# One change to the paged-decode phase of a two-layer decoder step: value products over two periods, low parts shared out anew, key and value loads in turn

## The reference, cut to what matters

```python
k_past = cache_k[page_table].reshape((db, past_len) + cache_k.shape[2:])
v_past = cache_v[page_table].reshape((db, past_len) + cache_v.shape[2:])
...
s = jnp.einsum('bqhcd,bkhcd->bhcqk', q, kp).astype(F32) * ATTN_SCALE
...
p = jax.nn.softmax(jnp.concatenate(scores, axis=-1), axis=-1)
w = p[:, :, 0] - lam * p[:, :, 1]
...
o = jnp.einsum('bhqk,bkhe->bqhe', w[..., start:start + s_len].astype(vp.dtype), vp)
```

## Time and profile before

| | us |
|---|---|
| median of 3 runs | 1853.9 (1852.12 to 1858.34) |
| the profiled execution's own time | 1853.4 |
| its span in the trace | 1851.5 |
| decode, from its first load to the next phase's first | 1446.7 to 1733.2 in the span |

### The profile page before, as it was taken

One profiled execution on the slowest core, in us unless ns is written; L12 is line 12 of the kernel. 1 busy time (PEld: TensorE's weight loads), 2 busy tenths in 40 slices (PEclk: granted clock), 3 DMA queues, 4 the chain that ended last, 5 costly groups with the idle time before them and its releaser, 6 DMA issues. The chain is left out here.

```text
span 1851.5 us, 31191 instructions
## 1 busy us (share of the span) xinstructions
PE 1684.9 (91%) x9243; PEld 1371.8 (74%) x9243; DVE 1041.6 (56%) x2696; ACT 839.0 (45%) x1994; POOL 319.6 (17%) x814
## 2 busy tenths in 40 slices
PE   5299999999999997988999999999999688887798
PEld 4288888888888876768878778778788566665576
DVE  4534445445454443354777767767766477776443
ACT  5333444344443332242555545555545366666322
POOL 1011212212112120010122221222222012111101
PEclk8599999999999998998999999999999799899799
DMA  6122050350421104322221211211101577877713
GB/s 167 27 58 69 27 94 2 92 94 0 94 49 44 38 2 143 100 83 66 58 57 44 66 54 37 61 54 43 43 12 35 187 253 250 293 239 249 264 53 112
DMA packets 164757, 171.97 MB, mean 93 GB/s; under 512 B 14634, under 2 KB 133834, under 8 KB 164658
## 3 DMA queue, kind: packets, MB, share of 16 engines
q1 hardware_dynamic: 161538, 170.78, 31.1%
q10 hardware_dynamic: 3120, 0.01, 0.1%
HBM read 141.85 MB, written 28.91 MB: 92 GB/s over the span
## 5 line engine op out<-in xcount | busy, mean ns | idle before, releaser
L1016 PE MATMUL PS<-WH,XH 128*128 128x512 f32 x512 | 212.5, 415 | 0.0
L1016 PE MATMUL PS<-WH,XL 128*128 128x512 f32 x512 | 201.9, 394 | 0.0
L1016 PE MATMUL PS<-WL,XH 128*128 128x512 f32 x512 | 201.9, 394 | 0.0
L1996 PE MATMUL PS<-W,XH 128*128 128x512 f32 x384 | 123.8, 403 | 0.0
L1750 ACT ACTIVATE WORK<-PD,WORK 128x896 f32<-128x896 f32 (+7 forms) x128 | 95.0, 742 | 62.8 <-DVE WORK L1917 57.9
L1016 PEld LDWEIGHTS PS<-WH,XL 128*128 128x128 f32 x512 | 96.2, 188 | 22.9
L1016 PEld LDWEIGHTS PS<-WH,XH 128*128 128x128 f32 x512 | 96.8, 189 | 19.8
L1016 PEld LDWEIGHTS PS<-WL,XH 128*128 128x128 f32 x512 | 96.8, 189 | 17.2
L1916 DVE TENSOR_REDUCE WORK<-PD 128x1 f32<-128x896 f32 (+7 forms) x128 | 96.4, 753 | 4.2 <-issue 2.0
L1996 PE MATMUL PS<-WH,XH 128*128 128x512 f32 (+2 forms) x224 | 85.7, 383 | 3.1 <-ACT WH L1715 3.1
L843 DVE SCALAR_TENSOR_TENSOR WORK<-PS,WORK 128x128 f32<-128x128 f32 (+1 forms) x72 | 20.1, 279 | 119.6 <-PE PS L1042 118.4
(11 more groups left out here) (365 smaller groups left out, 4663.5 us busy)
## 6 DMA issues: line engine op xcount, KB each, us to landing
RAW<-in_cache_k SPq DMA_DIRECT2D x64, 512.0 KB, 4.7
WORK<-in_cache_v SPq DMA_DIRECT2D x64, 512.0 KB, 4.5
RAW<-in_w_in_a SPq DMA_DIRECT2D x40, 512.0 KB, 7.3
out<-WORK SPq DMA_DIRECT2D x16, 512.0 KB, 3.0
out<-RAW SPq DMA_DIRECT2D x16, 512.0 KB, 3.2
RAW<-in_w_in_b SPq DMA_DIRECT2D x60, 128.0 KB, 2.4
RAW<-in_w_kv SPq DMA_DIRECT2D x56, 128.0 KB, 2.3
WORK<-d_G SPq DMA_DIRECT2D x8, 528.0 KB, 12.2
```

Source lines behind the costliest of these rows:

```text
L1016: last = nc.tensor.matmul(bank, x[:, k, tok(t, P)], wkvoz(w)[:, k, :], start=(k == i == 0), stop=(k == KT - 1 and i == 2))
L1996: last = nc.tensor.matmul(out, x[:, k, at(NT - 1 - s)], w[:, k, cols], start=(k == i == 0), stop=(k == KT - 1 and i == 2))
```

## The change

TensorE, ScalarE and VectorE get orders of their own. TensorE multiplies value pages 0 to 3 of batch b - 1 in period b, as before, and pages 4 to 7 and the new values only in period b + 1, between the turns of that period; so there is one more, short period at the end. ScalarE cuts the value pages between the key pages, from the period's start, and takes the result out in the middle of a period. GpSimd makes the low parts of pages 0, 2, 3, 4, 6 and 7, VectorE those of 1 and 5. The rota of banks has W after turn 7 and not after turn 9. SyncE loads keys and values in turn, page by page. The page table is loaded in the gates phase instead of at the start of decode, and the first eight key loads no longer wait for the small turns at decode's start (the inputs of these turns land in value places instead of the key places' tile).

```diff
@@ gates_phase, block.sync
+                    sp.dma_start(PT[:, :], page_table.rearrange("b n -> (b n)").unsqueeze(0)).then_inc(g_st, 16)
...
-                        sp.wait_ge(g_st, 64)
+                        sp.wait_ge(g_st, 80)
@@ decode_phase
-            TURNS = [u for u in range(10)] + ["W"] + [u for u in range(10, 16)]
+            TURNS = [u for u in range(8)] + ["W"] + [u for u in range(8, 16)]
...
+            ON_DVE = (1, 5)
+            ON_POOL = tuple(p for p in range(PAGES) if p not in ON_DVE)
+            def low_made(eng, i, p):
+                group, s = (ON_DVE, vld) if p in ON_DVE else (ON_POOL, vl)
+                wait(eng, s, len(group) * i + group.index(p) + 1)
+            PE_ORDER = ("T0", "V4", "V5", "T1", "V6", "T2", "V7", "N", "T3", "S0", "W", "S1",
+                        "T4", "V0", "T5", "V1", "T6", "V2", "T7", "S2", "V3", "S3")
+            ACT_ORDER = ("Q", "K0", "V0", "E", "K1", "V1", "K2", "V2", "K3", "V3", "O", "W",
+                         "K4", "V4", "K5", "R0", "V5", "K6", "V6", "K7", "R1", "V7", "R2")
+            DVE_ORDER = ("Q", "K0", "K1", "E", "V1", "K2", "K3", "W", "K4", "R0", "V5", "K5", "K6", "K7", "R1", "R2", "M")
...
-                body(0, True, False)
-                with eng.Fori(1, DB) as b:
+                body(0)
+                body(1)
+                with eng.Fori(2, DB) as b:
...
-                body(DB, False, True)
+                body(DB)
+                body(DB + 1)
@@ block.sync
-                    sp.dma_start(PT[:, :], page_table.rearrange("b n -> (b n)").unsqueeze(0)).then_inc(d_pt, 16)
-                    for j, dst in enumerate((RAW[0:TS, 4 * D - D:4 * D], RAW[0:TS, 4 * D:5 * D], AVS[0:TS, :])):
+                    for j, dst in enumerate((VB[0:TS, 2, :], VB[0:TS, 3, :], AVS[0:TS, :])):
...
-                    sp.wait_ge(d_pt, 16)
-                    sp.wait_ge(pre, 1)
...
+                    def body(b):
+                        for p in range(4, PAGES):
+                            keys(b, p)
+                            values(b - 1, p)
+                        if has_rest(b):
+                            store(b - 2)
+                        for p in range(4):
+                            keys(b + 1, p)
+                            values(b, p)
@@ block.gpsimd
-                        for p in (3, 7):
+                        for p in ON_POOL:
@@ block.scalar, v_high
-                            wait(act, av, PAGES * i + max(p - 3, 0))
+                            wait(act, av, PAGES * i + p - 3)
...
+                        def outputs():
+                            act.wait_ge(avd, i)
+                            wait(act, d_avs, 16 * (i - 1))
@@ block.tensor
-                        def value(p):
+                        def value(j, p):
+                            low_made(pe, j, p)
...
+                            elif step[0] == "V" and int(step[1]) < 4 and has_weights(b):
+                                value(i, int(step[1]))
+                            elif step[0] == "V" and int(step[1]) >= 4 and has_rest(b):
+                                value(i - 1, int(step[1]))
```

More of the change, by code:

```diff
@@ L2150, in sequences, with has_keys, has_weights @@
                     if links:
-                        links.enter(b - 1, per)
-                    body(b, True, True)
+                        links.enter(b - 2, per)
+                    body(b)
                 if links:
-                    links.leave(DB - 1)
-                body(DB, False, True)
+                    links.leave(DB - 2)
+                body(DB)
+                body(DB + 1)
+            def has_keys(b):
+                return not isinstance(b, int) or b < DB
+            def has_weights(b):
+                return not isinstance(b, int) or 1 <= b <= DB
@@ L2157, in wait, with has_rest @@
+            def has_rest(b):
+                return not isinstance(b, int) or b >= 2
             def wait(eng, s, count):
@@ L2179, in keys, with values @@
                           .then_inc(k_ld[p % 4], 16)
[L2181 to L2188, removed]
+                    def values(i, p):
+                        if p >= 4:
+                            low_made(sp, i, p - 4)
+                        else:
+                            low_made(sp, i - 1, p + 4)
                         src = cache_v[page(sp, i * PAGES + p), :, :, :]
@@ L2202, in _ @@
                         keys(1, p)
[L2203 to L2213, removed]
+                        if p == 2:
+                            sp.wait_ge(pre, 1)
+                        values(0, p)
+                    body(1)
+                    with sp.Fori(2, DB - 1) as b:
+                        body(b)
                     for p in range(4, PAGES):
                         keys(DB - 1, p)
-                    for p in range(4, PAGES):
                         values(DB - 2, p)
-                    for p in range(4):
+                    store(DB - 3)
+                    for p in range(PAGES):
                         values(DB - 1, p)
                     store(DB - 2)
-                    for p in range(4, PAGES):
-                        values(DB - 1, p)
                     for t in range(NT):
@@ L2246, in _, with body @@
                     act.wait_ge(ini, 2)
-                    def body(b, keys, values):
+                    def body(b):
                         i = b - 1
@@ L2307, in body @@
                             last.then_inc(avc, 1)
+                        for step in ACT_ORDER:
+                            if step[0] == "K" and has_keys(b):
+                                k_high(int(step[1]))
+                            elif step[0] == "R" and has_keys(b):
+                                low_rows(int(step[1]))
+                            elif step == "Q" and has_keys(b):
+                                queries()
+                            elif step == "E" and has_weights(b):
+                                exponentials()
+                            elif step == "W" and has_weights(b):
+                                weights_high()
+                            elif step[0] == "V" and has_weights(b):
+                                v_high(int(step[1]))
+                            elif step == "O" and has_rest(b):
+                                outputs()
                     sequences(act, body)
```

109 lines of the change are left out of this document (38 added, 71 removed).

## The result

The changed kernel takes 1867.9 us (median of 4 runs, 1867.29 to 1870.33) against 1855.4 us for the kernel before beside it (4 runs, 1852.12 to 1858.34). The ratio is 1.0074 [1.0057, 1.0091]: slower by 0.7%. The profiled execution took 1867.3 us with a span of 1865.5 us, 14.0 us more than the span of before. Medians take in every run; in two experiments one run was far slower than the rest (5718.9 us in experiment 1, 9197.2 us in experiment 5), and the ratios leave it out.

A forecast was written before the change was run, and what follows sets the result against it. The bound was taken as a ring TensorE, ScalarE, VectorE, TensorE, not an engine's sum. 7 x (32.0 - 30.9) + 7 x 0.4 - 3.0 - 2.5 = +5.0 on 1853.4: 1858 us; own range 1850 to 1866, whole 1835 to 1869.

The forecast's parts named there:

- Lows moved, the new wait: Steady period: with four low parts off VectorE, K5 queues behind R0 and V5; TensorE stands 3.3 us in T6; period 29.9.
- GpSimd beside VectorE: Query cuts wait for GpSimd's subtraction of V0; TensorE stands 3.3 us in T1; 2.1 us more a period, making 32.0.
- Rival 1: VectorE's query cuts don't wait for GpSimd; no clock term; 1839 us, chance 0.27.
- The period at full clock: One steady decode period without half clock: 32.0 us forecast, against 30.9 before the change.
- Clock: TensorE's half clock behind stalls, 0.8 us a period before; 0.4 more forecast, bounds 0 and rival 3's price.
- rival 3: Clock falls behind both T1 and T6 stalls, half clock as long as each stall; +2.5 us a period; 1873, chance 0.16.
- the sign: For rival 3: over half the periods show clock dips behind both stalls.
- Start and loads: Decode's start: earlier key loads and turns, net -3.0 us, between -4 and -1; no later load late, at nothing.
- End: From the last score to the result's copy: 28.2 us falls to about 25.7; net -2.5, between 0 and -5.
- the relief: VectorE loses four value pages' low parts, 4.6 us a period; by the walk seven periods gain only 7 us.
- the ring: Decode's waiting loop, TensorE to ScalarE to VectorE to TensorE, claimed as the bound; period 30.9 us with 5.7 of stalls.

The follow-up runs named there:

- experiment 1: The changed kernel with the exponential ahead of value page 0's cut on ScalarE; 1856.6 us, ratio 1.0008.
- experiment 5: The changed kernel with VectorE's query cuts behind the cuts of the first two key pages; 1845.1 us, ratio 0.9943.
- experiment 2: The changed kernel with VectorE cutting key pages 5 and 6 before value page 5; 1836.7 us, ratio 0.9896.
- experiment 4: The changed kernel with GpSimd filling value page 0's low part with zeros, all but one column not subtracted; 1845.5 us, ratio 0.9945.
- experiment 3: The changed kernel with 28 idle transposes ahead of each of TensorE's waits in T1 and T6; 1844.7 us, ratio 0.9943.
- experiment 8: The kernel before with 13 idle transposes ahead of each of its waits in T1 and T2; 1847.0 us, ratio 0.9958.
- experiment 9: The kernel before with only the change's earlier start of decode; 1851.8 us, ratio 0.9983.

## Why the prediction was right or wrong

The forecast was "just no change", +5.0 us and 1858; the profiled executions differ by +13.9, and the kernel is slower by 0.7%, 1868. That is inside the whole range (1835 to 1869), but 2 us outside the forecast's own (1850 to 1866). It went its way, with one term far too small and another on the cautious side, which by luck took back a third of it.

- **Lows moved, the new wait: right.** A stall of 3.3 us in T6's second half, K5 behind R0 and V5 on VectorE: 3.32 measured, and experiment 2 takes it away with the order alone.
- **GpSimd beside VectorE: right.** The query cuts wait for V0 (2.39 to 2.54 a pair), the T1 stall is 3.33 for 3.3. The collision had been bounded by 0 and 2.1 a period; in experiment 4, where no order changes, the stall is 1.48 instead of 3.33, so it is worth 1.9, and the period falls by 3.1 since the clock gives back the rest. Experiments 4 and 5 show that it needs GpSimd's reading and VectorE's two inputs in SBUF, and that size excuses nothing. Rival 1 falls.
- **The period at full clock: 32.0 forecast, 31.4 measured (experiment 3).** Both stalls have the forecast length, so it is TensorE's own work that was counted 0.4 to 0.6 too high: eight transposes of a key page, priced at 0.9, take 0.79 in the row (T0 of 1508.90, V4 starts at 1509.69). 7 x 0.6 = 4.2 us on the cautious side.
- **Clock: the step that failed**, the term of the sum that was too small. I wrote "I add half as much again, 0.4". Measured: 3.0 in the changed kernel (experiment 3) less 0.8 before (experiment 8), +2.2 a period. 7 x 1.8 = 12.6 us. The upper bound was the price in rival 3, +2.5, and the truth lies next to it. The reason given there, as long at half clock as the stall lasted, comes to 3.3 a period for 3.0 measured; windows behind 12 of the 13 stalls at 0.50 to 0.62 show the dip, and five of the six periods that have both stalls have both dips, the sign that the prediction had set for this rival. Scaling the 0.8 of before by half was too little: the stalls grew from 3.1 to 6.6 us a period, 2.1 times, and what the clock cost grew 3.7 times. Rival 3, to which I gave 0.16, is what happened (1873 by its sum, against 1867.3: 4.2 of the 5.8 is the period at full clock, 7 x 0.3 the clock itself).
- **Start and loads: right.** -3.15 for -3.0, -2.6 alone (experiment 9); between 1477 and 1720 every wait of TensorE that the profile lists (48.8 us in all) was released by a key cut, none by a load or by the result's copy.
- **End: right in size**, -2.1 for -2.5. GpSimd's pair of V2 and V3 also caught the weights' cut of 32 x 32, which takes 2.32 us in the last period; that was not foreseen.
- **The sum.** 5.0 + 12.6 - 4.2 - 0.15 + 0.4 = 13.7, and 14.0 is measured between the spans.

Where the gain of the relief went: VectorE had 4.6 us a period less to do, but the two operations on which the ring turns, the first key cut and K5's, each came later than before.

## What to carry over

Work moved to GpSimd is not free for VectorE: look at which VectorE operations have both inputs in SBUF, however small, and place GpSimd's reading beside operations that have one in PSUM or reduce a single tile; here the same work gives 1868 or 1809 us by nothing but the order of steps. When a step is moved out of a queue, walk the queue again for the operation on the ring, since what it gains by a shorter queue it can lose by one step that is now in front of it. And price a stall of TensorE with what comes behind it: two stalls of 3.3 us cost 6.6 us of waiting and 3.0 us of half clock.

## What the runs showed of the hardware

- Half clock behind stalls: 3.0 us a period for two stalls of 3.3 (experiment 3), 0.8 for two of 1.5 (experiment 8), so 0.45 us for each us of stall in the one case and 0.26 in the other.
- Idle transposes ahead of a wait pay: 23 us on the changed kernel with 392 of them, 7 us on the kernel before with 182, and the turns behind the waits start no earlier.
- Beside a subtraction of GpSimd an operation on 64 x 1 numbers, 0.15 us by itself, takes up to 0.60 us (experiment 1), and one of 32 x 32, 0.17 by itself, 2.32 (the changed kernel); fills by GpSimd (0.52 us for 511 columns) did not hold back the query cuts (experiment 4).
